# A 16-bit key search with a third step per block, and reordered short blocks, in the attention stage of a two-layer decoder step

## The reference, cut to what matters

```python
def _indexer_select(qi, wi, ki, qpos, topk):
    s = jnp.einsum('bqhd,bsd->bqhs', qi, ki) * (IDX_DIM ** -0.5)
    score = jnp.einsum('bqhs,bqh->bqs', jax.nn.relu(s), wi * (IDX_HEADS ** -0.5))
    score = jnp.where(causal[None], score, -jnp.inf)
    _, idx = lax.top_k(score, topk)
    ...
```

## Time and profile before

| | |
|---|---|
| median of 3 runs | 1838.53 us (1838.23 to 1842.24) |
| the profiled execution | 1841.42 us, its span 1839.6 us |
| mean granted TensorE clock | 0.989 of full speed |
| busy share of the span | PE 96%, DVE 79%, ACT 51%, POOL 23% |
| the attention, by the trace | from 527 to 656 us of the span |

### The profile page before, as it was taken

One profiled execution on the slowest core, in us unless ns is written; L12 is line 12 of the kernel. 1 busy time (PEld: TensorE's weight loads), 2 busy tenths in 40 slices (PEclk: granted clock), 3 DMA queues, 4 the chain that ended last, 5 costly groups with the idle time before them and its releaser, 6 DMA issues.

```text
span 1839.6 us, 36078 instructions
## 1 busy us (share of the span) xinstructions
PE 1767.8 (96%) x14199; PEld 1694.6 (92%) x14199; DVE 1452.0 (79%) x2177; ACT 931.7 (51%) x1464; POOL 422.6 (23%) x312
## 2 busy tenths in 40 slices
PE   7999999999998798999999999999999899999997
PEld 7999999987975498999999989999999799999996
DVE  5988887675988537988887598888876898888875
ACT  4455563353358726555562275555523565556333
POOL 3100044262220545000043230000543320002430
PEclk9999999999999999999999999999999999999998
DMA  5663423236210241334323324333233223433231
GB/s 170 191 201 95 114 87 104 87 100 141 53 56 1 67 136 52 104 103 114 94 89 100 108 69 115 102 103 115 87 96 105 59 62 99 113 107 99 83 102 47
DMA packets 275473, 180.74 MB, mean 98 GB/s; under 512 B 9366, under 2 KB 271902, under 8 KB 274845
## 3 DMA queue, kind: packets, MB, share of 16 engines
q1 hardware_dynamic: 266071, 158.50, 30.1%
q0 software_dynamic: 2144, 13.04, 2.0%
q10 hardware_dynamic: 7150, 7.70, 1.8%
HBM read 169.56 MB, written 8.08 MB: 97 GB/s over the span
## 4 chain that ended last, share of the span: by engine, by line
PE 74%; DVE 15%; ACT 6%; issue 3%; DMA 1%; POOL 0%; SPq 0%; ACTq 0%; DVEq 0%; POOLq 0%
PE ps L1371 41%; PE ps L1250 15%; PE ps L1434 9%; PE ps L1494 2%; DVE w_lo L1954 2%; PE ps L1499 1%; DVE q_lo L2639 1%; ACT xh L749 1%; ACT xf L751 1%; ACT p_t L886 1%; PE ps L1271 1%; DVE w_lo L2532 1%; ACT sc L864 1%; DVE q_sum L2716 1%; DVE xf L2004 1%
## 5 line engine op out<-in xcount | busy, mean ns | idle before, releaser
L2803 POOL TENSOR_TENSOR hl<-hid_all,hh 128x520 fp32r<-128x520 f32 x56 | 98.1, 1783 | 748.5 <-ACT hh L1110 748.5
L1040 ACT CAST w_hi<-w_sum 128x1024 fp32r<-128x1024 f32 x160 | 167.9, 1050 | 114.6 <-DVE w_sum L2514 107.2
L2532 DVE TENSOR_TENSOR w_lo<-w_sum,w_hi 128x1024 fp32r<-128x1024 f32 x160 | 194.6, 1218 | 4.5 <-ACT w_hi L1040 4.5
L1250 PE MATMUL ps<-hh,w_hi 128*128 128x260 f32 x896 | 191.6, 284 | 2.0 <-DVE w_lo L1954 2.0
L1250 PE MATMUL ps<-hh,w_lo 128*128 128x260 f32 x896 | 189.1, 282 | 0.0
L1371 PE MATMUL ps<-t_hi,w_hi 128*128 128x260 f32 x640 | 161.6, 284 | 0.7 <-DVE w_lo L2532 0.3
L1371 PE MATMUL ps<-xh,w_hi 128*128 128x260 f32 x640 | 159.9, 282 | 0.8 <-DVE w_lo L2532 0.8
L1371 PE MATMUL ps<-t_hi,w_lo 128*128 128x260 f32 x640 | 160.7, 283 | 0.0
L1371 PE MATMUL ps<-xh,w_lo 128*128 128x260 f32 x640 | 159.5, 283 | 0.0
L1250 PEld LDWEIGHTS ps<-hh,w_hi 128*128 128x128 f32 x896 | 145.3, 188 | 2.9 <-issue 2.7
L1250 PEld LDWEIGHTS ps<-hh,w_lo 128*128 128x128 f32 x896 | 145.6, 188 | 0.2
(11 more groups left out here) (375 smaller groups left out, 5235.9 us busy)
## 6 DMA issues: line engine op xcount, KB each, us to landing
w_raw<-in_ffn_wi_dram SPq DMA_DIRECT2D x176, 512.0 KB
w_raw<-in_ffn_wo_dram SPq DMA_DIRECT2D x16, 1024.0 KB
w_raw<-in_ffn_wo_dram SPq DMA_DIRECT2D x32, 512.0 KB
w_raw<-in_ffn_wo_dram SPq DMA_DIRECT2D x16, 768.0 KB
w_raw<-in_attn_w_in_dram SPq DMA_DIRECT2D x8, 1024.0 KB
keys_scratch<-key_half POOLq DMA_DIRECT2D x2, 2048.0 KB, 8.5
w_raw<-in_attn_w_o_dram SPq DMA_DIRECT2D x4, 1024.0 KB
x_in<-in_x_prompt_dram ACTq DMA_DIRECT2D x4, 512.0 KB, 9.8
```

The costliest lines, as they stand in the source:

```text
L1040: nc.scalar.copy(blocks(st, j)[1][0][:, x], w_sum[:, c % 2, x]).then_inc(s_sums_hi, 1)
L1250: mm = nc.tensor.matmul(ps[0:mc, bank + 2 * m + h, 0:HT], w[:, k, m, 0:mc], x(k)[:, h * HT:(h + 1) * HT], start=first and k == 0 and w is ...
L2532: nc.vector.tensor_tensor(lo[:, x], w_sum[:, (st.chunk + j) % 2, x], hi[:, x].bitcast(F32), ALU.subtract).then_inc(s_sums_lo, 1)
L2803: nc.gpsimd.tensor_tensor(hl[:, k, :], hid_all[:, k, :], hh[:, k, :].bitcast(F32), ALU.subtract).then_inc(s_hl, 1)
```

## The change

Three things change, all in the attention.

1. **The key search.** The scores are turned into integers whose order is the scores' order (`ordered`, once), and split into a high and a low half of 16 bits. Six units search the high half, then `low_keys` makes a 16-bit key of the low half, and six units search that; `threshold` puts the halves together. The compare (`test`) reads 16-bit integers and writes bf16, with candidates outermost; before, it read f32. `take` has two instructions where it had four. The sign step is gone, so there are 12 units and still 18 steps of DVE.
2. **A third side step** in blocks 1 to 5, on DVE behind the second, on PE behind `probs(B)`. The steps now end in block 7, where they ended in block 9. The gathers are placed at GpSimd's block 6 instead of 8, and still wait for `idx_sb`.
3. **Short blocks.** From block 8 on (`SHORT`), DVE takes `row_maxima(B, 0)` ahead of `inverse(B-1)` and `out_low` behind `row_maxima(B, 1)`; ACT makes all four heads' exponentials ahead of any copy; and the multiplication by the reciprocals (`normalised`) goes from four ACT instructions to one of DVE in `inverse`. In the blocks from 12 on `out_high` comes ahead of the second `sample_keys`.

```diff
-STEPS = (28, 25, 22, 19, 16, 13, 10, 7, 4, 1, 0)
-UNITS_OF = len(STEPS)
+SHIFTS = 2 * (13, 10, 7, 4, 1, 0)
+UNITS_OF = len(SHIFTS)
+HIGH_UNITS = UNITS_OF // 2
...
-        SIDES = UNITS_OF + 4
+        SIDES = UNITS_OF + 3
-        GATHERS = {8: 4 * DEC}
+        GATHERS = {6: 4 * DEC}
+        THIRD = range(1, 6)
+        SHORT = LATE - N_KV
+        SCALED = SHORT
...
                         exponentials(B, 0)
+                        if B >= SHORT:
+                            exponentials(B, 1)
                         if B > LATE:
                             sample_keys(2 * (B - LATE) - 1)
                         probs_out(B - 1, 0)
-                        exponentials(B, 1)
+                        if B < SHORT:
+                            exponentials(B, 1)
                         probs_out(B - 1, 1)
+                    if B >= 2:
+                        out_high(B - 2)
                     if B >= LATE:
                         sample_keys(2 * (B - LATE))
-                    if B >= 2:
-                        out_high(B - 2)
-                    normalised(B)
+                    if B < SCALED:
+                        normalised(B)
                     if B == LATE + 1:
                         split_hi(st.chunk)
...
-                        if 1 <= n <= UNITS_OF:
+                        if n < UNITS_OF:
                             for c in range(NC):
-                                mm = nc.tensor.matmul(ps[:, 6, 0:DEC * 7], ones_bf[:], tests[:, c].rearrange("p b j -> p (b j)"),
+                                mm = nc.tensor.matmul(ps[:, 6, 0:DEC * 7].rearrange("p (j b) -> p j b", b=DEC), ones_bf[:], tests[:, :, c, :],
...
                     if B >= 1:
                         probs(B)
+                    if B in THIRD:
+                        side_step()
...
+                def ordered():
+                    bits, order_i = order[:].bitcast(I32), order_sign[:]
+                    step(nc.vector.memset(reach[:, 0, :, 0], -32768.0))
+                    done(step(nc.vector.tensor_scalar(order[:], scores, 0.0, None, ALU.add)))
+                    done(step(nc.vector.tensor_scalar(order_i, bits, 31, 1, ALU.arith_shift_right, ALU.logical_shift_right)))
+                    done(step(nc.vector.tensor_tensor(bits, bits, order_i, ALU.bitwise_xor)))
+                    done(step(nc.vector.tensor_scalar(bits, bits, 32768, None, ALU.bitwise_xor)))
+                    done(step(nc.vector.tensor_copy(key[:], half_keys(1))))
+                def half_keys(part):
+                    return order[:].bitcast(I16).rearrange("p b (n t) -> p n b t", t=2)[:, :, :, part]
...
-                    units = cst("unit")[:, 7 * k:7 * k + 7].bitcast(I32)
-                    n = step(nc.vector.tensor_tensor(cand[:], thr[:].unsqueeze(2).broadcast_to([P, DEC, 7]),
-                                                     units.unsqueeze(1).broadcast_to([P, DEC, 7]), ALU.bitwise_xor))
-                    done(n)
-                    nc.vector.tensor_tensor(tests[:], scores.rearrange("p b n -> p n b").unsqueeze(3).broadcast_to([P, NC, DEC, 7]),
-                                            cand[:].bitcast(F32).unsqueeze(1).broadcast_to([P, NC, DEC, 7]), ALU.is_ge)\
-                      .then_inc(s_hits, 1)
+                    units = cst("unit")[:, 7 * k:7 * k + 7].unsqueeze(2).broadcast_to([P, 7, DEC])
+                    done(step(nc.vector.tensor_tensor(cand[:], reach[:, k % 2, :, 0].unsqueeze(1).broadcast_to([P, 7, DEC]), units, ALU.add)))
+                    nc.vector.tensor_tensor(tests[:], key[:].unsqueeze(1).broadcast_to([P, 7, NC, DEC]),
+                                            cand[:].unsqueeze(2).broadcast_to([P, 7, NC, DEC]), ALU.is_ge).then_inc(s_hits, 1)
                 def take(k):
-                    widths = 7 if STEPS[k] else 1
-                    dve.wait_ge(s_cnt, k + 2)
-                    at_ = step(nc.vector.tensor_scalar(reach[:], ps[:, 6, 0:DEC * 7].rearrange("p (b j) -> p b j", b=DEC), float(TOPK_D),
-                                                       None, ALU.is_ge))
-                    done(at_)
-                    at_ = step(nc.vector.tensor_reduce(need[:], reach[:, :, 0:widths], AX.X, ALU.add))
-                    done(at_)
-                    at_ = step(nc.vector.tensor_tensor(delta[:], need[:], cst("unit")[:, 7 * k:7 * k + 1].bitcast(I32).broadcast_to([P, DEC]),
-                                                       ALU.mult))
-                    done(at_)
-                    at_ = step(nc.vector.tensor_tensor(thr[:], thr[:], delta[:], ALU.bitwise_xor))
-                    done(at_)
+                    widths = 7 if SHIFTS[k] else 1
+                    new = half_thr[:, k // HIGH_UNITS, :] if SHIFTS[k] == 0 else reach[:, (k + 1) % 2, :, 0]
+                    dve.wait_ge(s_cnt, k + 1)
+                    done(step(nc.vector.tensor_scalar(reach[:, k % 2, :, 1:8], ps[:, 6, 0:DEC * 7].rearrange("p (j b) -> p b j", b=DEC),
+                                                      float(TOPK_D), float(1 << SHIFTS[k]), ALU.is_ge, ALU.mult)))
+                    done(step(nc.vector.tensor_reduce(new, reach[:, k % 2, :, 0:1 + widths], AX.X, ALU.add)))
+                def low_keys():
+                    step(nc.vector.memset(reach[:, 0, :, 0], -32768.0))
+                    done(step(nc.vector.tensor_tensor(distance[:], key[:], half_thr[:, 0, :].unsqueeze(1).broadcast_to([P, NC, DEC]),
+                                                      ALU.subtract)))
+                    done(step(nc.vector.scalar_tensor_tensor(distance[:], distance[:], 65536.0, half_keys(0), ALU.mult, ALU.add)))
+                    done(step(nc.vector.tensor_scalar(key[:], distance[:], 32767.0, -32768.0, ALU.min, ALU.max)))
+                def threshold():
+                    halves_of = thr[:].bitcast(I16).rearrange("p (b t) -> p b t", t=2)
+                    step(nc.vector.tensor_copy(halves_of[:, :, 1], half_thr[:, 0, :]))
+                    done(step(nc.vector.tensor_copy(halves_of[:, :, 0], half_thr[:, 1, :])))
+                    done(step(nc.vector.tensor_scalar(thr[:], thr[:], 32768, None, ALU.bitwise_xor)))
+                    done(step(nc.vector.tensor_scalar(thr_sign[:], thr[:], 31, 1, ALU.arith_shift_right, ALU.logical_shift_right)))
+                    done(step(nc.vector.tensor_tensor(thr[:], thr[:], thr_sign[:], ALU.bitwise_xor)))
...
-                        nc.vector.tensor_scalar(hits[:], scores, 0.0, None, ALU.is_ge).then_inc(s_hits, 1)
+                        ordered()
-                    elif n <= UNITS_OF:
-                        take(n - 2)
-                        test(n - 1)
-                    elif n == UNITS_OF + 1:
+                    elif n < UNITS_OF:
+                        take(n - 1)
+                        if n == HIGH_UNITS:
+                            low_keys()
+                        test(n)
+                    elif n == UNITS_OF:
                         take(UNITS_OF - 1)
+                        threshold()
...
                 for B in range(1, len(BLOCKS)):
-                    if B > 1:
+                    if 1 < B < SHORT:
                         inverse(B - 1)
-                    if B >= 3:
+                    if 3 <= B < SHORT:
                         out_low(B - 3)
                     if B >= 2:
                         dve.wait_ge(s_tp, tile_base[B - 1])
                     row_maxima(B, 0)
+                    if B >= SHORT:
+                        inverse(B - 1)
                     if B == 1:
                         inverse(0)
                         rope_sin(*TILES[-1])
                         page_scores(DEC - 1)
                     side_step()
                     row_maxima(B, 1)
+                    if B >= SHORT:
+                        out_low(B - 3)
                     side_step()
+                    if B in THIRD:
+                        side_step()
...
-                nc.vector.reciprocal(row_inv[:, B % 2, :], row_sum[:, B % 2, :]).then_inc(s_rinv, 1)
+                x = nc.vector.reciprocal(row_inv[:, B % 2, :], row_sum[:, B % 2, :])
+                if B < SCALED:
+                    x.then_inc(s_rinv, 1)
+                else:
+                    n = (BLOCKS[B][0] + 1) * P
+                    rows = (sc if B < LATE else sc_late)[:, 1 - B % 2, :, 0:n]
+                    done(step(x))
+                    nc.vector.tensor_tensor(rows, rows, row_inv[:, B % 2, :].unsqueeze(2).broadcast_to([P, 4, n]), ALU.mult).then_inc(s_p, 2)
```

More of the change, by code:

```diff
@@ L12 @@
 BF16 = mybir.dt.bfloat16
+I16 = mybir.dt.int16
 ALU = mybir.AluOpType
@@ L88, in constants @@
     out["iota"] = np.tile(np.arange(16.0), (P, 1))
-    unit = np.array([[j << u if u or j == 1 else 0 for j in range(1, 8)] for u in STEPS], np.int32).reshape(1, -1)
-    out["unit"] = np.tile(unit.view(np.float32), (P, 1))
+    out["unit"] = np.tile(np.array([[j << u if u else 1 for j in range(1, 8)] for u in SHIFTS], f).reshape(1, -1), (P, 1))
```

(30 more changed lines are left out.)

7 lines of the change are left out of this document (2 added, 5 removed).

## The result

The changed kernel took 1848.59 us (median of 5 runs, 1847.77 to 1851.17) against 1838.64 for the kernel before, a ratio of 1.0053 (95% interval 1.0043 to 1.0064). It is slower by 10 us. I had said no change, 1838.9, and a range up to 1848.0. The profiled execution took 1847.77 with a span of 1845.6.

What follows compares the result with a forecast made beforehand. No engine is full; the attention is set by how engines wait for one another. Early blocks lose 13.8 us, late ones win 13.4, sum +0.35: from the median 1838.53 to 1838.9 us, range 1830.5 to 1848.

Steps and rivals of the forecast that it cites:

- A compare and a step: DVE's search step: compare of 952 elements takes 0.65 us instead of 1.15, a step costs DVE 1.31.
- Block 1, +2.2: Block 1: `ordered` adds 1.3 to 1.6, a third step 1.3, cheaper compare returns 0.5 to 0.9; block 2 starts 2.2 later.
- Blocks 2 to 5: Three-step blocks: third count stands behind the last transposes, second step is covered; blocks take 10.85, 11.35, 9.8 and 9.05 us.
- the rival on PE's clock: Three-step blocks: PE's clock falls to its lower level, 2.1 us a block, 5.2 for two and a half, 1843.9; chance 0.18.
- Blocks 6 and 7: Ranks, slots and one-hot product (3.4): 10.4 and 9.2 us; block 8 starts 13.8 us later than before.
- Blocks 8 to 15, the gain: Short blocks: loop of 4.25 us, later 4.85 with sample steps; late blocks win 13.4 us.
- Gathers near 603 instead of 610.77, worth nothing: Gathers start near 603 instead of 610.77 us, gaining nothing since nobody waited for them.
- my +0.35: Whole attention: early blocks lose 13.8 us, late ones win 13.4, sum +0.35.
- the late blocks' rival: Late blocks win more, as waits vanish, `split_hi` hides and the one-hot matmul finds full clock: 1833.4 us; chance 0.29.

Runs made afterwards that it cites:

- search_alone: The kernel before with only the new search, two steps a block and the old late-block order; 1839.67 us, ratio 1.0001 to the kernel before.
- third_step: The changed kernel with the late blocks ordered as before, so new search and third step only; 1850.54 us, ratio 1.0057 to the kernel before.
- start_warm: The changed kernel plus unread PE products, 8 ahead of each wait of block 0's transposes and 10 ahead of the first count; 1848.51 us.
- two_warm: The changed kernel without the third step, gathered values awaited by fours, 40 unread products ahead of the one-hot product; 1837.03 us, 0.9981 of the kernel before.
- two_all: two_warm plus the unread products of start_warm at block 0 and the first count; 1836.49 us, ratio 0.9983 to the kernel before.
- three_double_count: three_all with every count of the search done twice; 1849.32 us, ratio 1.0061 to the kernel before.
- scores_first: The changed kernel with PE's second scores of a short block ahead of the values of the block two before; 1849.53 us, ratio 1.0047.
- warm: The changed kernel plus 24 unread products in PE's wait ahead of the one-hot product; 1846.66 us, ratio 1.0044 to the kernel before.
- short_order: The changed kernel without the third step, gathers from block 8: new search and short-block order only; 1844.28 us, ratio 1.0019 to the kernel before.
- three_all: two_all with the third step in blocks 1 to 5, gathers at block 6, 24 unread products instead of 40 ahead of the one-hot product; 1846.42 us.
- maxima_first: The changed kernel with block 1's second maxima ahead of the first search step; 1849.32 us, ratio 1.0054 to the kernel before.

## Why the prediction was wrong

Two steps failed. The early blocks were to lose 13.8 us and lost 19.1; 2.2 of the miss stand in block 1, where both `ordered` and the third step cost more than their own instructions, and most of the rest in block 3 and block 7. The late blocks were to win 13.4 and won 10.5, above all because their loop was summed to 4.25 and takes 4.88. By the prediction's own steps, from block 0's reciprocal:

- **A compare and a step**: right, 0.66 for 0.65.
- **Block 1, +2.2**: it was +4.4, the largest miss of the early blocks. The runs split it. The block takes 8.69 before, 10.47 in `search_alone`, 12.89 in `third_step` and 13.11 in the change. So `ordered` less the cheaper compare costs 1.8, where I had 0.4 to 1.1, and the third step 2.4 to 2.6, where I had a step of DVE, 1.3. Of the second, 0.8 is the clock: `start_warm` has 12.30. The clock was as low before, but with two steps the block is no longer for it (10.45 in `two_warm` at 0.62, 10.46 in `two_all` at 1.00). Of the first, 1.5 stands beside POOL (0.66 + 1.33 for what takes 0.21 + 0.23 without it). I had taken the length of `ordered` from short rows with no POOL beside them, and had not asked why the old `hits` took 0.68 at the same place. But taking this wait away alone gave nothing back, so the 1.5 is a reading of lengths and not a price shown.
- **Blocks 2 to 5**: 11.2, 12.8, 9.6, 9.5 against 10.85, 11.35, 9.8, 9.05. The chain was right, and `three_double_count` agrees that one of three counts costs nothing. Block 3 is 1.0 and block 5 0.45 longer than in `third_step`, which had a clock of 1.00 there. This is the rival on PE's clock, at a quarter of its price of 5.2. It is also a matter of the execution: up to block 5 `third_step`, `scores_first`, `warm` and the change run the same code, and block 3 took 11.82, 11.83, 12.20 and 12.80 in them, block 5 9.02 in all but the change's.
- **Blocks 6 and 7**: 10.5 for 10.4, and 10.2 for 9.2, the one-hot product being 3.81 instead of 3.4. Block 7's reciprocal, which I took for block 8's start, came 19.1 later, not 13.8.
- **Blocks 8 to 15, the gain**: mis-sized by 2.95. Until block 9's copy 15.5 instead of 14.45, then three blocks 1.25 more with a period of 4.88 instead of 4.25, and blocks 12 to 15 0.65 more. I had summed busy times of a circle and left out most of the time between engines.
- **Gathers near 603 instead of 610.77, worth nothing**: they came 2.7 earlier, counted from block 0's reciprocal, and were worth nothing here. But the claim that they are no bound held only for an attention as long as that. `short_order` shows it.

Together 2.2 + 0.35 + 1.45 - 0.15 + 0.4 + 0.1 + 0.95 + 2.95 = 8.25 more than my +0.35, which is the 8.6. The other 1.4 us of the medians' 10 I have not placed; the interval of the ratio, 7.9 to 11.8 us, has room for 8.6. All misses but one had one sign. My terms were sums of durations, most of them at the full clock and on undisturbed engines, so an omission made the chain longer, while the forecast was a difference of two sums of 13 us. The recorded text has three slips that change nothing: the first gather starts 3.7 us behind the end of the one-hot product, not 6; the multiplication of block 4 starts 0.6 after the reciprocal in the earlier trace rows, not 0.3 (in the trace of after 0.22); and 1838.9 + 5.2 is 1844.1, not 1843.9. The rival on the clock had the right direction, and the late blocks' rival was wrong: the steps taken out of blocks 8 and 9 were nearly free there once the order of these blocks was changed. From block 7's reciprocal to block 9's copies `three_all` wins back only 3.8 of 15.1 us on `two_all`.

## What to carry over

A step that is a round trip between two engines should stand where another chain covers it; here a third one in a block put two of three in series, and the blocks that it left did not pay it back. When a change shortens a stage, look at who arrives at its end at the same time, and at what the change puts beside it: here the gathers, issued later and wanted earlier, turned 2.3 us won into 4 lost, until the wait was split. And when a forecast is the difference of two large sums, widen it on the side of the omitted gaps.

## What the runs showed of the hardware

A DVE instruction on two elements, 0.17 us long in most places, took 0.77 us beside POOL in `maxima_first` and 0.95 in the change at 589.37. It ends when POOL's instruction does, to 0.03 us. In the change, in block 3:

```profile
557.71 0.71 DVE L2158 TENSOR_SCALAR neg_max<-row_max 128x2 f32<-128x2 f32 x1
...
556.41 2.00 POOL L2920 CAST count<-const 128x2176 bf16<-128x2176 f32 x1 [19.36 <-DVE row_inv L2403]
```

It goes the other way too. In all the traces of this study, each issue of a gather above 1.11 us has one of DVE's products or differences of two tensors beside it, and ends 0.86 to 0.88 after it (0.96 or 0.97 in four cases where it is the first gather). The two pairs shown above are such: 651.53 + 2.71 is 0.87 behind 651.08 + 2.29, and 616.44 + 1.34 is 0.87 behind 615.68 + 1.23. The subtraction of weights was there before, but its second piece came behind the last gather (654.00 against 652.62). Moving it was not tried, nor giving the multiplication back to ACT.

And, in `warm`, 24 unread products in a wait of 2.6 us kept the granted clock at 1.00, the level of 2.4 GHz, and made the product behind it 2.03 instead of 3.81 long. They don't always hold it: in `three_all`, with the same products at block 0 as `start_warm`, the clock from 541 to 546 was 0.66.
